# Expert stage: gate and up weights of every expert loaded within the stage arrive as two 1 MB halves, each with a signal of its own

## The reference, cut to what matters

```python
scores = sigmoid(h @ w_router); 8 of 64 experts are chosen per token (group-limited), gates renormalised
act    = silu(h @ w_gate[e]) * (h @ w_up[e])          # 1024 -> 256, twice
routed = sum over chosen e of gates[e] * (act @ w_down[e])   # 256 -> 1024
shared = (silu(h @ sh_gate) * (h @ sh_up)) @ sh_down
h      = layer_norm(ALPHA * h + routed + shared)
```

## Time and profile before

| what | us |
|---|---|
| median of 3 runs | 1531.64 (1527.8 to 1534.02) |
| the profiled execution | 1535.17 |
| its span in the trace | 1533.3 |
| TensorE busy in the span | 1445.1 (94%) |
| packets of SyncE's queue, share of the 16 DMA engines | 79.5% |

### The profile page before, as it was taken

The page is one execution under the profiler, slowest core; times in us unless marked ns, Lnnn a source line. Parts: engine busy times, 40 slices in busy tenths (PEclk is TensorE's granted clock), DMA queues, the critical chain, the costliest instruction groups (busy, mean ns, idle before and its releaser), DMA issues. The chain is left out here.

```text
span 1533.3 us, 24378 instructions
## 1 busy us (share of the span) xinstructions
PE 1445.1 (94%) x9446; PEld 854.1 (56%) x9446; DVE 644.4 (42%) x1451; ACT 342.6 (22%) x714; POOL 249.6 (16%) x331
## 2 busy tenths in 40 slices
PE   8999998999899899999998889999979999999985
PEld 6888768987555455454454367874524444434431
DVE  2767458532532344343343259053233333333423
ACT  3766454310410111111111030142001111111101
POOL 5779625300100000000000000011000000000000
PEclk9999999899999999999999989999989999999998
DMA  7669562059599999999999973499999999999995
GB/s 284 219 189 227 183 169 68 2 199 352 207 417 425 424 422 424 421 420 420 418 425 422 411 302 142 167 386 365 419 423 425 423 424 420 416 409 424 424 420 229
DMA packets 106256, 512.38 MB, mean 334 GB/s; under 512 B 36996, under 2 KB 42180, under 8 KB 68508
## 3 DMA queue, kind: packets, MB, share of 16 engines
q1 hardware_dynamic: 96316, 481.75, 79.5%
q0 software_dynamic: 9824, 29.05, 5.0%
HBM read 508.85 MB, written 17.10 MB: 343 GB/s over the span
## 5 line engine op out<-in xcount | busy, mean ns | idle before, releaser
L1895 PE MATMUL banks<-upper,e_xgT 128*64 128x512 f32 (+1 forms) x880 | 195.3, 614 | 10.0 <-issue 5.9
L366 PE MATMUL banks<-hT,dense_ring 128*128 128x272 f32 x768 | 183.6, 397 | 5.0 <-DMA dense_ring<-in_w_in 5.0
L2104 DVE TENSOR_TENSOR e_ac<-e_sl,banks 128x256 f32<-128x256 f32 x54 | 22.8, 421 | 383.0 <-ACT e_sl L2022 383.0
L1470 POOL DMA_INDIRECT x_xg<-rows_dram,x_idx x54 | 53.7, 995 | 797.6 <-DVE x_idx L1462 781.5
L1895 PE MATMUL banks<-experts,e_xgT 128*64 128x512 f32 (+1 forms) x720 | 172.9, 614 | 6.9 <-issue 3.8
L366 PEld LDWEIGHTS banks<-hT,dense_ring 128*128 128x128 f32 x768 | 146.6, 192 | 38.3 <-DMA dense_ring<-in_w_in 5.0
L1895 PEld LDWEIGHTS banks<-upper,e_xgT 128*64 128x64 f32 (+1 forms) x880 | 65.5, 131 | 131.2 <-issue 131.2
L1895 PE MATMUL banks<-dense_ring,e_xgT 128*64 128x512 f32 (+1 forms) x288 | 126.8, 593 | 0.0
L2022 ACT ACTIVATE e_sl<-banks 128x256 f32<-128x256 f32 x54 | 20.8, 385 | 469.2 <-PE banks L1895 469.2
L1950 PE MATMUL banks<-dense_ring,e_aT 128*64 128x512 f32 (+1 forms) x304 | 113.4, 612 | 3.4 <-DVE acc L2076 2.8
L1895 PEld LDWEIGHTS banks<-experts,e_xgT 128*64 128x64 f32 (+1 forms) x720 | 56.9, 130 | 87.3 <-issue 87.2
(11 more groups left out here) (452 smaller groups left out, 2082.9 us busy)
## 6 DMA issues: line engine op xcount, KB each, us to landing
upper<-in_moe_gate_up SPq DMA_DIRECT2D x43, 2048.0 KB, 19.7
experts<-in_moe_gate_up SPq DMA_DIRECT2D x34, 2048.0 KB, 20.3
upper<-in_moe_down SPq DMA_DIRECT2D x43, 1024.0 KB, 17.9
experts<-in_moe_down SPq DMA_DIRECT2D x43, 1024.0 KB, 18.4
dense_ring<-in_moe_down SPq DMA_DIRECT2D x38, 1024.0 KB, 19.1
dense_ring<-in_moe_gate_up SPq DMA_DIRECT2D x18, 2048.0 KB, 20.9
upper<-in_moe_gate_up SPq DMA_DIRECT2D x24, 1024.0 KB, 18.3
dense_ring<-in_w_in SPq DMA_DIRECT2D x47, 512.0 KB, 5.3
```

The lines of the kernel that those rows point to most:

```text
L366: mm = pe.matmul(ps[g % 4][:, 0:T], slot[:, n % SLOTS_IN, c, :], hT[:, c, :], start=(c == 0), stop=(c == DC - 1))
L1470: pool.indirect_dma_start(out=ex["xg"][:, i % 2, :], out_offset=None, in_=mem["rows_dram"], in_offset=bass.IndirectOffsetOnAxis(ap=ex["idx ...
L1895: mm = pe.matmul(gub[e * n:(e + 1) * n, :], xgT[:, i % 2, c, e * n:(e + 1) * n], gate_up_weights(mem, j)[:, c, :], start=(c == 0), stop=(c ...
L2104: dve.tensor_tensor(ac[:], sl[:], gub[:, FF:], ALU.mult).then_inc(mul, 1)
```

## The change

`IN_HALVES` now holds every expert that is loaded within the stage but expert 13, so experts 14 to 59 (46 per layer) join 5 to 12 and 60 to 63. Nothing else in the file is touched; both forms of a load and both kinds of waits were there already.

```diff
@@ -100,7 +100,7 @@
 SHARED_NEXT = SLOT_OF.index(SHARED_SLOT)
 LAST_IN = (E - 2, E - 1)
-IN_HALVES = [j for i in range(SHARED_UNIT + 1) for j in LOADS[i] if j != SHARED_NEXT] + list(range(E - 4, E))
+IN_HALVES = [j for js in LOADS for j in js if j != SHARED_NEXT]
```

## The result

With halves the kernel takes 1543.38 us in the median of 10 runs (1539.03 to 1553.01), the kernel before 1532.76 us (1524.77 to 1536.43). The medians differ by 10.6 us. The ratio is 1.0077, with a 95% interval of 1.0055 to 1.0099, and by it the change costs 11.8 us, 8.4 to 15.2. So it is slower by more than 0.5%. The forecast was 1537.0 us and, as the likeliest case, "within 0.5%": the time lies in the range of 1528 to 1547 us, but what came is the case "slower", which had 0.28.

The account below looks back on a forecast made before the run. Each expert stage was taken to end when the last byte of an always full DMA queue lands. All terms were nothing except 5.4 us for loads in two pieces, added to the 1531.64 us median: 1537.0 us, range 1528 to 1547 us.

Parts of the forecast that it names:

- The bound: Both expert stages: the end is set by the last byte landing from an always full DMA queue, share 1.01.
- Earlier issue, nothing: Loads of experts 14 to 59: first halves issued 3.6 us earlier gain nothing, hidden by the queue's backlog.
- Place limit and issue instructions, nothing: SyncE's queue: a limit of about eight transfers, 92 more issues and a second TensorE wait cost nothing.
- Unit 24 begins earlier, unit 26 waits longer: Stage end, layer 0: unit 24's wait 5.87 to about 1 us, unit 26's 3.63 to 6 or 7; net nothing.
- The clock, 0: Unit 26's second half of gate_up: longer waits stretch it by 0, at most 2.7 us in all.
- The price of a piece: Loads of experts 14 to 59: two pieces cost 0.059 us more per load, 5.4 us over both layers.
- the sum: Whole kernel: the only nonzero term, 5.4 us for loads in two pieces, giving 1537.0 us, 0.35% more.
- Rival 1: Mid-stage queue: pieces cost more, slower; 2.51 us a piece adds 7.8 us, 2.56 us adds 17 us; chance 0.27.
- Rival 2: Ahead of unit 24: saved 4.9 and 3.8 us are kept, faster, 1522.9 us; chance 0.10.
- Rival 3: Load queue: each transfer's fixed part paid alone, 1.4 us times 92, 127 us, 1659 us; chance 0.01.
- Rival 4: Experts 14 to 59: the change doesn't do what it says; with other cases leaving the time as is, chance 0.02.
- The rule against the change: DMA loads: the skill's batching rule, about 2 us fixed per transfer, gives 184 us for 92 more; prediction disagreed.

Follow-up runs that it names:

- whole_two_runs: Kernel before, one DMA per load, but weights laid out in HBM as two blocks, so each load is 256 runs of 8 KB: 1537.87 us, 1.0032.
- whole_four_runs: Kernel before, one DMA per load, but weights laid out in HBM as four blocks, so each load is 512 runs of 4 KB: 1557.08 us, 1.0164.
- halves_late: Changed kernel with first halves of experts 14 to 59 held back until all of gate_up is done: 1543.17 us, 1.008 of the kernel before.
- halves_again: Changed kernel once more, unaltered, for a second profile: 1542.0 us, 1.008 of the kernel before.
- split_even_odd: Kernel before with each load of experts 14 to 59 cut into two DMAs, even and odd partitions, runs still 16 KB: 1531.78 us, 1.0014.
- halves_packed: Changed kernel with weights laid out so that each half lies in HBM without gaps: 1544.84 us, 1.0075 of the kernel before.
- whole_again: Kernel before once more, unaltered, for a second profile: 1531.89 us, 0.9988.
- halves_hold: Changed kernel with unit 24 held until all its gate and up weights and expert 56's down weights have come: 1540.21 us, 1.0042 of the kernel before.
- quarters: Changed kernel with each half of experts 14 to 59 moved by two DMAs of 64 neighbouring partitions, 512 KB apiece: 2157.7 us, 1.4053 of the kernel before.

## Why the prediction was right in part, and where it failed

**The bound, right.** The share stayed at 1.01 to 1.02, and from whole_two_runs to whole_four_runs, with no other edit than the length of the runs, the stages get longer as the last bytes come later.

**Earlier issue, nothing: right**, by halves_late against halves_again (1.008 both). **Place limit and issue instructions, nothing: right**, by split_even_odd, which issues as many DMAs and stays at 1.0014. (It has no second wait in gate_up; that one was not tested by itself.) SyncE was held for most of a transfer at some of them without harm; in a row of four halves its own timeline after reads

```profile
508.31 0.89 SPq L1246 DMA_DIRECT2D upper<-in_moe_gate_up  x1
509.39 2.00 SPq L1246 DMA_DIRECT2D dense_ring<-in_moe_gate_up  x1
511.57 2.00 SPq L1246 DMA_DIRECT2D upper<-in_moe_gate_up  x1
513.75 2.00 SPq L1246 DMA_DIRECT2D dense_ring<-in_moe_gate_up  x1
```

The last of these landed 28.3 us after its issue; at 2.48 us a piece that is, by an estimate, some eleven transfers in line, so my eight was low. The pieces in line are more, not fewer, which is the safe side.

**Unit 24 begins earlier, unit 26 waits longer: right in kind.** I said 5.87 to some 1 us in each of two parts, and 3.63 to 6 or 7 us. Ahead of unit 24 it was 2.98 us in layer 0 and 4.11 + 0.46 us in layer 1, and 5.07 us in layer 0 of halves_again. Within unit 26 it was 6.06 to 6.17 us in all eight waits of the four profiles with halves (after, halves_again, halves_late, halves_packed), against 2.16 to 3.63 us in the two with whole loads. The saving ahead of unit 24 is less steady than I had it; the two profiles with whole loads alone differ there by 2.5 us in layer 0.

**The clock, 0: right against the kernel before.** The second half of gate_up in unit 26 took 4.97 to 6.41 us in the four profiles with halves, against 6.50 and 5.34 us in the earlier trace rows and 5.34 twice in whole_again. What I didn't see is that later bytes can also move the wait away from there: whole_two_runs, with the same delay, did this half in 3.64 us and ends its stages 3.8 us ahead of the mean of the four profiles with halves (957.55 us). With halves TensorE can begin unit 24 sooner, runs ahead into unit 26 and waits there; halves_hold takes this wait away and ends its stages where whole_two_runs does. That this explains the difference in the timed runs is argued and not shown.

**The price of a piece: the step that failed.** I had 0.059 us a load, 5.4 us in all, and took it for the price of cutting a transfer in two. Two things were off.
- Its size. In the profiles of after, halves_again, halves_packed and halves_late the last bytes come 6.6, 7.0, 7.6 and 7.9 us later than with whole loads (both layers, against the mean of the two profiles), 0.071 to 0.086 us a load. The rows on which I had put it, give landings in tenths of a us for a difference of 0.06 us a load, and could not have told 5.4 from 7. At 7.0 us the sum alone would have stood just under the 7.7 us at which "within 0.5%" ends.
- Its cause. It is no cost of a transfer but of its runs: rows of 8 KB instead of 16 KB, some 0.55 ns for each packet more. I had set the down weights apart, as a lower bound, because they lie without gaps; in halves_packed the halves do too, and it gains nothing.

**What it missed beside that.** The stages of the four profiles with halves are 7.3 us longer than those of the two with whole loads (957.55 against 950.26 us), and the runs differ by 11.8 us (8.4 to 15.2). The rest of the span is 579 to 584 us in ten of the twelve profiles in the table; in two, after and halves_hold, it is 594 and 593 us. Both have the gather of unit 0 late, here in after:

```profile
416.61 1.97 PE L1874 MATMUL banks<-ident,x_xg 128*128 128x128 f32 x8 [5.93 <-DMA x_xg<-rows_dram,x_idx]
```

and both are 5.5 us behind the first profile of the kernel before already ahead of that, in layer 0's mixer, where no instruction of the change has run yet: TensorE's clock from 250 to 300 us is 0.81 in these two and 0.90 or more in the ten others. First before, then after:

```profile
250.00:300.00 50.00, 50.00 (x1083) 45.99 (x1079) 36.41 (x82) 17.49 (x57) 22.80 (x30) 0.90 0.01 3
```

```profile
250.00:300.00 50.00, 50.00 (x1090) 45.82 (x1086) 32.96 (x75) 17.46 (x57) 23.00 (x31) 0.81 0.01 3
```

Such executions don't explain the missing 4 us or so by being more frequent. If they did, the shorter runs would differ less than the longer ones, but the lower quartile, the median and the upper quartile of the 38 runs of the four kernels with halves all lie 11.8 to 11.9 us above those of the 101 runs of the kernel before (1541.4, 1543.4 and 1546.7 against 1529.6, 1531.6 and 1534.8 us). Over their whole span these runs have a mean granted clock of 0.972, the kernel before 0.974 to 0.975, so part of it may be time at the lower clock; but whole_two_runs has 0.972 too and costs only 4.9 us. Where the missing time lies stays open.

**The rivals.** Rival 1 (slower) had the right sign and, in its threshold of 2.51 us a piece, nearly the right size, but not its mechanism. The first and the last of the four halves issued at 508.31 to 513.75 us took, from issue to landing,

```profile
upper<-in_moe_gate_up SPq DMA_DIRECT2D x1, 1024.0 KB, 26.3
```

```profile
dense_ring<-in_moe_gate_up SPq DMA_DIRECT2D x1, 1024.0 KB, 28.3
```

so they landed at 534.6 and 542.05 us, three intervals of 2.48 us; nothing near 2.56 us in the middle of a stage. Rival 2 (faster) is refuted: the last bytes came later, not earlier. Rival 3 is refuted by split_even_odd. Rival 4 by the page, x100 of 1024 KB. The chances leaned too far to "same": the sum stood only 2.3 us below the 7.7 us that decide, and what I had named beside it (2.7 us of clock, more for a piece) lay mostly on the upper side. That the time fell into the range owes something to luck: the range went to 1547 us for a dearer piece in the middle of the stage, and what filled it is in part the missing time above.

**The rule against the change.** The rows after show a piece of 1 MB each 2.48 us, and split_even_odd has 92 transfers more at a ratio of 1.0014 with an interval that holds 1. The Trainium skill, DMA: Bandwidth & Descriptors, Anatomy of one DMA, has the fixed part of about 2 us for each DMA, fitted to DMAs that GpSimd issues; by it the prediction came to 184 us, an estimate, and the runs disagree for SyncE's queue that is always full. The Trainium skill's rule in the section Bandwidth of the same page asks for at least 1 MiB per DMA, which the halves still have, so it is no rule against this change.

## What to carry to other kernels

In this queue, which never ran dry, the number of transfers was free and the length of the contiguous runs was not: rows of 16 KB cut in two cost 0.07 to 0.09 us per 2 MB load, and cutting a load between partitions (even and odd) instead of along its rows cost nothing that shows. But try which partitions a piece takes: two pieces of 64 neighbouring ones halved the rate. A finer signal pays only if what it lets start early is not followed by a wait for the same last bytes; look at which wait ends the stage, and count what the earlier start moves into it. When a small term decides between two cases, take it from the whole stage of a run that has it (first matmul to last landing), not from a few landings read in tenths.

## What the runs showed that I had not expected

- A transfer over 64 neighbouring partitions runs at half the rate: 214 GB/s for loads in two such pieces and 236 GB/s for quarters, at DMA shares of 1.01 and 1.02, from 600 to 760 us, while in the same stretch the same bytes cut into even and odd partitions ran at 418 GB/s. What in the chip makes the difference these runs don't show.
- The rate falls with the run: from 440 to 820 us and from 1100 to 1460 us it is 421 to 422 GB/s in the three profiles with rows of 16 KB (before, whole_again, split_even_odd), 418 to 419 in the five with 8 KB (after, halves_again, halves_late, halves_packed, whole_two_runs) and 412 with 4 KB. Each packet more costs 0.56 to 0.58 ns at two very different counts.
- TensorE kept its full clock in the half of gate_up right behind waits of 1.12 to 1.53 us (3.64 us), in split_even_odd behind one of 2.29 us and in unit 24 of halves_packed behind waits of 2.43 to 3.26 us; behind waits of 2.13 to 6.17 us in other places the same 32 matmuls took 4.97 to 6.50 us. So between 2.1 and 3.3 us the length of the wait alone doesn't tell which it will be; what else decides I didn't test. In unit 26 the full clock wasn't quite free: behind the waits of 1.12 to 2.29 us the matmuls of down took 3.83 to 3.91 us in place of 3.64.
